# Splitting the attention rows, output product, residual, norm and router logits made one stage that runs row tile by row tile, with the parts of the weights held on chip

## The reference, cut to what matters

```python
def rmsnorm(x, g):
    xf = x.astype(jnp.float32)
    y = xf * lax.rsqrt(jnp.mean(xf * xf, axis=-1, keepdims=True) + EPS)
    return (y * g.astype(jnp.float32)).astype(x.dtype)

    # second layer, in reference()
    x = x + nsa_mixer(h, w_qg[j], g_q[j], w_o[j], rel_bias, *shared)   # ends with: return out @ w_o
    h = rmsnorm(x, norm_ffn[layer])
    x = x + moe(h, router[i], moe_wg[i], moe_wu[i], moe_wd[i])
    # moe begins with
    logits = jnp.einsum('nd,de->ne', xf, router, preferred_element_type=jnp.float32)
```

## Time and profile before

| what | us |
|---|---|
| median of 3 runs | 4501.77 (4493.52 to 4503.23) |
| the profiled execution | 4501.5 |
| its span (first to last instruction) | 4499.9 |
| TensorE busy, share of the span | 4073.3, 91% |
| VectorE busy | 2396.8, 53% |
| ScalarE busy | 1617.3, 36% |
| GpSimd busy | 500.8, 11% |

### The profile page before, as it was taken

One profiled execution on the slowest core, in us unless ns is written; L12 is line 12 of the kernel. 1 busy time (PEld: TensorE's weight loads), 2 busy tenths in 40 slices (PEclk: granted clock), 3 DMA queues, 4 the chain that ended last, 5 costly groups with the idle time before them and its releaser, 6 DMA issues. The chain is left out here.

```text
span 4499.9 us, 63874 instructions
## 1 busy us (share of the span) xinstructions
PE 4073.3 (91%) x22970; PEld 3510.4 (78%) x22970; DVE 2396.8 (53%) x3364; ACT 1617.3 (36%) x2189; POOL 500.8 (11%) x911
## 2 busy tenths in 40 slices
PE   6999999996996888877369999999999999999993
PEld 5888888885875555546369999999999999999983
DVE  4444544444433667642335555555566666666675
ACT  3222222222332566651123232333334444444452
POOL 2000000001222554320110000000000000000001
PEclk8999999998997899998589999999999999999997
DMA  6222232225454211112443343333345555545576
GB/s 232 103 103 93 103 123 92 103 75 205 132 148 133 80 61 40 40 61 87 159 151 139 116 160 116 140 146 144 144 182 193 194 193 193 195 178 209 187 285 247
DMA packets 171773, 639.18 MB, mean 142 GB/s; under 512 B 28624, under 2 KB 64848, under 8 KB 131411
## 3 DMA queue, kind: packets, MB, share of 16 engines
q1 hardware_dynamic: 148932, 563.70, 34.6%
q0 software_dynamic: 14896, 50.89, 3.0%
q10 hardware_dynamic: 7824, 23.07, 1.4%
HBM read 552.48 MB, written 85.12 MB: 142 GB/s over the span
## 5 line engine op out<-in xcount | busy, mean ns | idle before, releaser
L411 PE MATMUL moe_ps<-moe_ht_hi,moe_gu_hi 128*128 128x256 f32 (+2 forms) x3136 | 944.9, 301 | 1.3 <-DVE moe_ht_lo L305 1.3
L413 PE MATMUL moe_ps<-moe_ht_hi,moe_gu_lo 128*128 128x256 f32 (+2 forms) x3136 | 945.2, 301 | 0.0
L412 PE MATMUL moe_ps<-moe_ht_lo,moe_gu_hi 128*128 128x256 f32 (+2 forms) x3136 | 945.0, 301 | 0.0
L226 ACT CAST moe_gu_hi<-moe_gu_raw 128x2048 fp32r<-128x2048 f32 x226 | 431.3, 1908 | 586.9 <-PE moe_ps L413 504.0
L309 DVE TENSOR_TENSOR moe_gu_lo<-moe_gu_raw,moe_gu_hi 128x2048 fp32r<-128x2048 f32 x226 | 517.5, 2290 | 213.1 <-ACT moe_gu_hi L226 213.0
L411 PEld LDWEIGHTS moe_ps<-moe_ht_hi,moe_gu_hi 128*128 128x128 f32 x3136 | 596.1, 190 | 5.2 <-issue 1.7
L412 PEld LDWEIGHTS moe_ps<-moe_ht_lo,moe_gu_hi 128*128 128x128 f32 x3136 | 596.1, 190 | 3.5
L413 PEld LDWEIGHTS moe_ps<-moe_ht_hi,moe_gu_lo 128*128 128x128 f32 x3136 | 596.1, 190 | 0.0
L342 DVE TENSOR_TENSOR moe_yacc<-moe_yacc,moe_ps 128x512 f32<-128x512 f32 x504 | 344.1, 688 | 360.1 <-PE moe_ps L455 359.8
L453 PE MATMUL moe_ps<-moe_wd_hi,moe_hid_hi 128*128 128x512 f32 x1008 | 395.7, 393 | 0.0
L454 PE MATMUL moe_ps<-moe_wd_lo,moe_hid_hi 128*128 128x512 f32 x1008 | 393.5, 390 | 0.0
(11 more groups left out here) (315 smaller groups left out, 6830.4 us busy)
## 6 DMA issues: line engine op xcount, KB each, us to landing
moe_gu_raw<-in_moe_wgu SPq DMA_DIRECT2D x226, 1024.0 KB
moe_wd_raw<-in_moe_wd SPq DMA_DIRECT2D x112, 1024.0 KB, 6.7
ffn_gu_raw<-in_ffn_wgu SPq DMA_DIRECT2D x58, 1024.0 KB, 4.8
ffn_wd_raw<-in_ffn_wd SPq DMA_DIRECT2D x28, 1024.0 KB, 6.6
y_moe<-zeros SPq DMA_DIRECT2D x32, 512.0 KB, 3.0
kvq_raw<-in_w_kvq SPq DMA_DIRECT2D x10, 1024.0 KB, 7.6
kt_rows<-kvq_work SPq DMA_DIRECT2D x16, 512.0 KB, 3.2
qt<-kvq_work SPq DMA_DIRECT2D x16, 512.0 KB, 3.0
```

The source lines that it names most:

```text
L226: act.copy(gu_hi[s][:, :, :, :].rearrange("p a k c -> p (a k c)"), gu_raw[s][:, :]).then_inc(s_gu_hi, 1)
L411: pe.matmul(out[:, 0:W], gu_hi[s][:, half, k, :], ht_hi[:, k, 0:W], start=(k == 0), stop=False)
L412: pe.matmul(out[:, 0:W], gu_hi[s][:, half, k, :], ht_lo[:, k, 0:W], start=False, stop=False)
L413: last = pe.matmul(out[:, 0:W], gu_lo[s][:, half, k, :], ht_hi[:, k, 0:W], start=False, stop=(k == KT - 1))
```

## The change

`split_rows`, `project` and `add_norm` are deleted, and so is the device tensor `att_out`. One function, `project_out`, takes their place as one stage. It keeps both parts of all of `w_o` in SBUF (four raw buffers, `w_hi` and `w_lo` of 128x2x8x512) and goes over the 8 row tiles once. For a tile it loads 128 tokens of the attention rows (pieces of 512 bytes), splits them, multiplies by both chunks into two PSUM banks, adds `x1` straight from PSUM, norms, turns and multiplies by the router. In TensorE's stream the product of tile i stands ahead of the transposes of tile i-1 and the logits of tile i-2. The number of matmuls, their operands, their order within a sum and the number of transposes stay what they were. All loads and stores go through SP.

```diff
-        with ExitStack() as proj:
-            xt_hi, xt_lo = (sb(proj, f"ot_{n}", [P, KT, SEQ], F32R) for n in ("hi", "lo"))
-            split_rows(nc, ot_dram, xt_hi, xt_lo)
-            project(nc, "wo", xt_hi, xt_lo, w_o, None, 2, att_out)
...
-        add_norm(nc, "moen", x1, att_out, gain_ffn1, x2, h_moe, ident, router=router, logits=logits)
+        project_out(nc, ot_dram, w_o, x1, gain_ffn1, router, ident, x2, h_moe, logits)
...
+def project_out(nc, ot_rows, w_o, x1, gain, router, ident, x2_rows, h_rows, logits):
...
+        acc = [ctx.enter_context(nc.psum_tensor(f"out_acc{s}", [P, D], F32)) for s in range(2)]
+        t_ps = ctx.enter_context(nc.psum_tensor("out_t", [P, KT, P], F32))
...
+        @block.sync
+        def _(sp):
+            def load(i):
+                if i >= 2:
+
+                    sp.wait_ge(s_otlo, i - 1)
+                sp.dma_start(ot[i % 2][:, :, :], ot_rows[:, :, i * P:(i + 1) * P]).then_inc(s_ot[i % 2], 16)
+                if i >= 2:
+                    sp.wait_ge(s_x2, i - 1)
+                sp.dma_start(xt[i % 2][:, :], rows(x1, i)).then_inc(s_x[i % 2], 16)
...
+            load_weights(0)
+            load(0)
+            for n in range(1, 4):
+                load_weights(n)
+            load(1)
+            sp.dma_start(g[:, :], broadcast_rows(gain, D)).then_inc(s_g, 16)
+            sp.dma_start(r[:, :, :], router.rearrange("(k p) e -> p k e", p=P)).then_inc(s_r, 16)
+            for i in range(TILES):
+                sp.wait_ge(s_x2, i + 1)
+                sp.dma_start(rows(x2_rows, i), x2[i % 3][:, :]).then_inc(s_x2_out[i % 3], 16)
+                if i + 2 < TILES:
+                    load(i + 2)
+                sp.wait_ge(s_h, i + 1)
+                sp.dma_start(rows(h_rows, i), ht[i % 2][:, :]).then_inc(s_h_out[i % 2], 16)
...
+        @block.scalar
...
+            weights_hi(0)
+            rows_hi(0)
+            for n in range(1, 4):
+                weights_hi(n)
+            rows_hi(1)
+            for i in range(TILES):
+                act.wait_ge(s_x2, i + 1)
+                if i:
+                    act.wait_ge(s_sq, i)
+                act.activation(squares[:, :], x2[i % 3][:, :], ACT.Square, accum_out=ss[:, i:i + 1]).then_inc(s_sq, 1)
+                if i + 2 < TILES:
+                    rows_hi(i + 2)
+                if i:
+                    turned(i - 1)
+            turned(TILES - 1)
...
+        @block.vector
...
+            dve.wait_ge(s_g, 16)
+            for i in range(TILES):
+                dve.wait_ge(s_mm, i + 1)
+                dve.wait_ge(s_x[i % 2], 16 * (i // 2 + 1))
...
+                dve.tensor_tensor(x2[i % 3][:, :], acc[i % 2][:, :], xt[i % 2][:, :], ALU.add).then_inc(s_x2, 1)
+                if i + 2 < TILES:
+                    rows_lo(i + 2)
+                dve.wait_ge(s_rs, i + 1)
...
+                dve.scalar_tensor_tensor(out=ht[i % 2][:, :], in0=x2[i % 3][:, :], scalar=rs[:, i:i + 1], in1=g[:, :],
+                                         op0=ALU.mult, op1=ALU.mult).then_inc(s_h, 1)
+                if i >= 2:
+                    take_logits(i - 2)
...
+        @block.tensor
+        def _(pe):
+            def multiply(i):
+                pe.wait_ge(s_otlo, i + 1)
+                if i >= 2:
+
+                    pe.wait_ge(s_x2, i - 1)
+                s = i % 2
+                for c in range(2):
+                    out = acc[s][:, c * C:(c + 1) * C]
+                    for k in range(KT):
+                        if i == 0 and k % HK == 0:
+                            pe.wait_ge(s_wlo, c * 2 + k // HK + 1)
+                        pe.matmul(out, ot_hi[s][:, k, :], w_hi[:, c, k, :], start=(k == 0), stop=False)
+                        pe.matmul(out, ot_hi[s][:, k, :], w_lo[:, c, k, :], start=False, stop=False)
+                        last = pe.matmul(out, ot_lo[s][:, k, :], w_hi[:, c, k, :], start=False, stop=(k == KT - 1))
+                last.then_inc(s_mm, 1)
...
+            pe.wait_ge(s_r, 16)
+            for i in range(TILES):
+                multiply(i)
+                if i >= 1:
+                    turn(i - 1)
+                if i >= 2:
+                    route_logits(i - 2)
+            route_logits(TILES - 2)
+            turn(TILES - 1)
+            route_logits(TILES - 1)
```

More of the change, by code:

```diff
@@ L2160, in _, with weights_lo @@
         @block.vector
         def _(dve):
-            for k in range(KT):
-                dve.wait_ge(s_hi, k + 1)
-                dve.tensor_tensor(xt_lo[:, k, :], raw[k % 4][:, :], xt_hi[:, k, :], ALU.subtract).then_inc(s_lo, 1)
+            def weights_lo(n):
+                c, half = divmod(n, 2)
+                part = (slice(None), c, slice(half * HK, (half + 1) * HK))
+                dve.wait_ge(s_whi, n + 1)
+                dve.tensor_tensor(w_lo[part], w_raw[n][:, :, :], w_hi[part], ALU.subtract).then_inc(s_wlo, 1)
@@ new lines, in rows_lo, with take_logits @@
+            def rows_lo(i):
+                dve.wait_ge(s_othi, i + 1)
+                dve.tensor_tensor(ot_lo[i % 2][:, :, :], ot[i % 2][:, :, :], ot_hi[i % 2][:, :, :], ALU.subtract).then_inc(s_otlo, 1)
+            def take_logits(i):
+                dve.wait_ge(s_l, i + 1)
+                dve.tensor_copy(logits[:, i:i + 1, :], l_ps[i % 2][:, :].rearrange("p (a e) -> p a e", a=1)).then_inc(s_logits, 1)
+            weights_lo(0)
+            rows_lo(0)
+            for n in range(1, 4):
+                weights_lo(n)
@@ new lines, in _, with turn, route_logits @@
+            take_logits(TILES - 2)
+            take_logits(TILES - 1)
+        @block.tensor
+        def _(pe):
+            def multiply(i):
+                pe.wait_ge(s_otlo, i + 1)
+                if i >= 2:
+                    pe.wait_ge(s_x2, i - 1)
[9 more added lines that the diff above has]
+                last.then_inc(s_mm, 1)
+            def turn(i):
+                pe.wait_ge(s_h, i + 1)
+                if i:
+                    pe.wait_ge(s_hT, i)
+                for k in range(KT):
+                    last = pe.transpose(t_ps[:, k, :], ht[i % 2][:, k * P:(k + 1) * P], ident)
+                last.then_inc(s_t, 1)
+            def route_logits(i):
+                pe.wait_ge(s_hT, i + 1)
+                if i >= 2:
+                    pe.wait_ge(s_logits, i - 1)
+                for k in range(KT):
+                    last = pe.matmul(l_ps[i % 2][:, :], hT[i % 2][:, k, :], r[:, k, :], start=(k == 0), stop=(k == KT - 1))
+                last.then_inc(s_l, 1)
+            pe.wait_ge(s_r, 16)
+            for i in range(TILES):
+                multiply(i)
+                if i >= 1:
+                    turn(i - 1)
+                if i >= 2:
+                    route_logits(i - 2)
+            route_logits(TILES - 2)
+            turn(TILES - 1)
+            route_logits(TILES - 1)
```

333 lines of the change are left out of this document (60 added, 273 removed).

## The result

The changed kernel took 4433.2 us (median of 4 runs, 4429.91 to 4437.89) against 4497.65 us for the kernel before (4 runs, 4492.67 to 4503.23). The ratio of the times is 0.9855, with a 95% interval of 0.9842 to 0.9868, so it is faster by 1.3 to 1.6%. The forecast was 4439, its range 4427 to 4458. The profiled execution took 4429.91 us, its span 4428.4, 71.5 less than the 4499.9 of before.

The account below looks back on a forecast made before the run. Stages in series, not an engine, were taken to bound the stretch. Terms 22.1 + 13.4 + 76.3 + 15.4 + 0.4 + 11.0 = 138.6 us replace 201.45, so 4501.8 - 62.8 = 4439 us; range 4427 to 4452, 4458 with a late load.

Parts of the forecast that it names:

- head: From the new stage's first issue to the first matmul, waiting for the router, last of ten transfers: 22.1 us.
- first tile: Product of tile 0, its first twelve matmuls slow at 5.25 us, then 36 at 0.227: 13.4 us.
- products: Matmuls of the other seven tiles, 48 each at 0.227 us: 10.9 us a tile, 76.3 us in all.
- turns and logits: Six tiles' transposes and five tiles' router products between the matmuls, at clock 1.00: 15.4 us.
- wait: TensorE's wait for normed rows h, ready 11.3 us behind the product: 0.4 us, in the first tile only.
- tail: From the last product's end to routing's first issue: 11.0 us, or 16.1 us at clock 0.50.
- Outside the stage: Attention ahead, routing and experts behind, 4298.5 us of span: untouched, counted at zero change.
- Clock falling between products: Rival: TensorE's clock drops to 0.50 at each of six tile boundaries and in the tail; 4472 us, chance 0.07.
- Load late: Rival: each tile's attention rows land late, so TensorE waits for h; 4445 to 4463 us, chance 0.09.
- Norm not hidden: Rival: TensorE waits for each tile's own norm, 19.9 us a tile, stage 185; 4485 us, chance 0.03.
- the slow rival: Rival: the clock never rises in the new stage, 384 matmuls at 0.4375 us, stage 233; 4533 us, chance 0.03.

Follow-up runs that it names:

- The two halves of the change: Split folded under the products, but norm and logits left as the old separate stage behind: 4487.33 us, against 4433.2 for the full change.
- the late router: Changed kernel, but TensorE waits for the router only ahead of the first logits, not the first product: 4429.7 us, ratio 0.9839 to the kernel before.
- the warm head's run: The early-start kernel plus 70 unused transposes ahead of the first product: 4424.69 us, ratio 0.9835 to the kernel before.
- The own-norm kernel: Changed kernel, but TensorE takes each tile's transposes and logits right behind that tile's own product: 4551.51 us, stage 249.1 us.
- the early-start kernel: Changed kernel with router wait moved to the first logits, attention rows loaded first, x1 last, 14 unused transposes in the tail: 4422.87 us, ratio 0.9829.

## Why the prediction was right

**The sum.** The stage came out at 135.9 us where I had 138.6. The terms missed by -2.1 (head), -0.7 (first tile), -0.6 (products), -0.5 (turns and logits), -0.4 (wait) and +1.5 (tail), so part of the closeness is errors that cancel. Of the 5.8 us between 4439 and 4433.2, 4.1 lie in the kernel before: I had subtracted from 4501.8, and its median beside the result is 4497.65. The ends of the forecast's own range, 4427 and 4452, aren't the sum of its terms either, which gives 4435 to 4453; 4433.2 lies below that, by the change in the kernel before.

**The bound.** I had put the stretch down to stages in series and not to an engine. The two halves of the change, 17.7 and 47.8 us, with the middle of the new stage 100% TensorE, show it.

**Head, 22.1 forecast, 20.0 measured.** The mechanism was right: of the waits, the first product's is for the router.

Waits of the changed kernel, in the stage: in total, times, longest; then SP's issues in the head.

```profile
PE out_acc L2000 <- DMA out_r<-in_router: 23.3, 1, 23.3
```

```profile
2013.82 6.70 SPq L1873 DMA_DIRECT2D out_x<-x  x1
2020.56 1.47 SPq L1885 DMA_DIRECT2D out_g<-in_gain_ffn  x1
2022.08 0.44 SPq L1886 DMA_DIRECT2D out_r<-in_router  x1
```

SP was held for 6.70 us on the second load of x1, and issued the router only at 2022.08, 12.8 us in; it landed 7.1 us later. What I had as 6.81 MB at mixed rates moved at 343 GB/s over the whole head [windows above], start included, so 2.1 us less than my sum and within its lower end of 19. The low part of the last weights was done at 19.8, 0.2 ahead of the first matmul, where I had counted 1.6 of cover. The experiment with the late router puts the price of that wait at 6 to 8 us of the stage: a dependency of the first product on the last byte of a queue that the first product doesn't need.

The key loads' peaks in the earlier trace rows run from 303 to 344 GB/s, where I wrote 315 to 344. On small pieces the Trainium skill (DMA: Bandwidth & Descriptors, Specifications) allows line rate from 512 bytes up. By the page I would have come 0.5 us nearer; but the head's 343 GB/s is a mean over a mixed queue, which doesn't tell the 512-byte pieces from the long ones.

**First tile, 13.4 and 12.7; products, 10.9 and 10.82.** The first matmuls of the product behind the idle stretch ran at the slow level, eight loads of 0.28 to 0.33 us where I had twelve slow matmuls; from then on a matmul takes 0.23 us, as the earlier trace rows had it.

**Turns and logits, 15.4 and 14.9.** The distances from 2042.03 to 2132.67 sum to 90.64 us; seven bare products of 10.82 are 75.7, which leaves 14.9. The bounds for the logits were 1.77 and 3.54 at a tile; they are 1.86 to 1.87. The clock was 1.00 at each boundary.

**Wait for h, 0.4 forecast, none in one profiled execution and 0.45 in the other.** I had the load landing 7.7 us behind the product and h at 11.3. In the execution read above ScalarE starts on the loaded rows 5.8 to 6.7 us behind the add, and h was there after 9.4 to 10.2 us in the six tiles with a load. The cover is 0.9 us in the first tile, where I had -0.4, 1.3 in the second, and 3.0 to 3.8 in the next four, where I had 2.5. (I had 2.5 for the second as well, but no logits stand ahead of its due time: by my own terms it is 0.96 + 10.9 - 11.3 = 0.6.) In the changed kernel's second profiled execution the same steps end between 9.6 and 11.9 us behind the add, and TensorE waited for the first h.

TensorE's load of the first turn in the repeated run of the changed kernel.

```profile
2052.58 0.86 PEld L2011 LDWEIGHTS out_t<-ident,out_h 128*128 128x128 f32 x8 [0.45 <-DVE out_h L1980]
```

So the argument was right and its size near; how far the rows' load is behind the add changes by up to 2 us from execution to execution, for a reason that these runs don't show.

**Tail, 11.0 and 12.5.** Up to logits 7 the steps came as reckoned: from the product's end they begin at 7.9 us in both. Then they loaded for 3.49 us and not 1.9.

TensorE's loads in the tail of the changed kernel: logits 6, turn 7, logits 7.

```profile
2136.03 1.86 PEld L2020 LDWEIGHTS out_l<-out_r,out_hT 128*128 128x128 f32 x16 [0.93 <-ACT out_hT L1927]
2137.73 1.29 PEld L2011 LDWEIGHTS out_t<-ident,out_h 128*128 128x128 f32 x8
2140.53 3.49 PEld L2020 LDWEIGHTS out_l<-out_r,out_hT 128*128 128x128 f32 x16 [1.50 <-ACT out_hT L1927]
```

The clock fell within turn 7 (1.29 us, 1.02 in the tiles before), so behind the gap of 0.93 us and ahead of that of 1.50. I had priced a slow tail at up to 5 us and put it in the range; what was wrong is that I took either level for the entire tail, where it falls part way. That the price is the clock's is shown by the filled tail, 10.6 us with all loads at full clock. When and why it falls is open: with the late router it was down one step earlier, for logits 6, behind the same gap, and in the warm head's run it fell in turn 7 with the gaps filled.

**Outside the stage.** I counted it at zero. The stage began at 2009.28 and not 2013.99, 4.7 us that are part of the 71.5 in the spans, and 1.3 more came behind it. In the kernels of this study, whose code ahead of the stage is the same, it began between 2009.1 and 2014.1, so this is scatter of the attention stage and none of the change; the medians differ by 64.5 us, near the stage's 65.5.

**The rivals.** *Clock falling between products:* not in the changed kernel, clock 1.00 in every tile. The Trainium skill (TensorE: Matmul & The Clock Gate, HAM oscillation) has the clock fall at each contraction tile of a kernel that waits for a transfer at each. The changed stage has no such wait, so I was wrong to say that it would be this rival by that rule. The own-norm kernel waits at each tile, for h, and its clock did fall (mean granted clock 0.71 over the stage, logits at 3.49 us a tile); where unused transposes filled the waits, the first two tiles ran at granted clock 1.00. *Load late:* not here, real with more transfers; I had priced it at seven tiles, and six have a load. *Norm not hidden:* I gave it 19.9 us a tile, 185 in all, 4485. At full clock it is 20.0, so the sum was right for what was in it; but it left out the 5.1 us of the load chain and the 4.6 of the clock that such a wait brings, and the case is 4551.5, slower than the kernel before. The faster-or-slower question of this change thus hung on the order of TensorE's stream more than I had said: the slow rival that I worked out had every matmul at the slow level, and the one that the runs can produce is a product at full clock behind a wait, a late load chain and a slow start. It did not touch the forecast, since the stream was there to be read.

## What to carry to other kernels

When stages are joined, ask first which engine's own instructions are the floor, then put every other tile's chain under that engine's next long block; the same joined stage without the late turn was slower than the stages apart. A wait inside such a block is to be priced three times: its length, what else stands ahead of the producer on its engine (here a load chain ahead of the norm, 5.1 us), and the clock that falls while TensorE waits (4.6 us). Both figures are of one tile of one run. Then look at the two ends: a first matmul that waits for a late and unneeded transfer (6 us here), and a tail in which the clock can fall, so that the last logits take twice their price.

## What the runs showed of the hardware that I hadn't expected

- The clock fell in the tail within 6 us of the last product, from turn 7 on in the changed kernel and the warm head's, from logits 6 on with the late router (last logits 3.49, 2.42 and 3.49 us in place of 1.86). With 14 unused transposes in the tail it stayed up in one run and not in another. With 24 of them a tile the norm stage of before ran at 0.96 in its steady part, where it had run at 0.50.
- SP's queue held one issue for 6.70 us with 5.8 MB issued ahead of it, part of which had landed (7.89 us for two issues behind 5.2 MB in the early-start kernel), while the changed kernel's other single issues took 0.3 to 1.5 us. A transfer's place in the queue thus also sets when it is issued, not only when it lands.
- Reading x1's partner from PSUM costs VectorE nothing: the 128x1024 add takes 1.23 us (mean 1225 ns of eight), and the same add in the norm stage of before, with both operands in SBUF, took 1224 ns. I had allowed 0.1 us more.
- A further 0.52 MB transfer ahead of the rows delayed them by 1.6 us with three of them and 1.4 with six, little more than the 1.3 that I had from its bytes.
